# Reading the moving operand of every product in sixteens from the end, with the split weights at other addresses

## The chip, the cores and the metric

One core of a Trainium2 chip. The metric is the device time of one execution of the whole program, in microseconds; the kernel is one launch.

## The reference

Two transformer blocks for one sequence of 256 tokens and width 2048, in fp32. The first has modulation from a condition vector, a gated linear recurrence in two directions with 8 heads (after a pass over a context of 256 tokens that yields its starting states), a short gated convolution beside it, a gated merge, an output projection, and a feed-forward of width 5632 with a 3 x 3 depthwise convolution on a 64-wide grid. The second has 16 extra leading tokens (so 272), eight heads of stick-breaking attention and eight of differential attention, and an output projection. In outline:

```python
mod = silu(c) @ w_mod + b_mod
h = modulate(rms_norm(x), sh1, sc1)
z = h @ w_in                      # q, two forget gates, v, g, conv and merge gates
o = recurrence(z)                 # both directions, states from the context
merged = sigmoid(ga) * (y_a @ w_pa) + sigmoid(gb) * (y_b @ w_pb)
x = x + g1 * (merged @ w_o)
a, b = split(modulate(rms_norm(x), sh2, sc2) @ w_up)
x = x + g2 * ((silu(dwconv(a)) * b) @ w_down)
x = rms_norm(x) * final_g
proj = rms_norm(concat(meta, x)) @ w_in_2
x = x + concat(stick_breaking(proj), diff_attention(proj)) @ w_out_2
```

## The kernel before

All activations are kept with the features on the 128 partitions and the tokens along the free axis. Every large matrix is cut into units of 128 output features: one unit is 16 blocks of 128 x 128 weights (11 in the stage down), 1 MB, fetched by one DMA of the sync queue into one of four places of RAW. A unit becomes one **product**: for each of its 16 blocks three matmuls accumulate into one bank of ACC. The three are needed because an fp32 number is split in two parts of a faster type (fp32r), a high and a low one: ScalarE copies the high part of the weights from RAW to HI (line 488), VectorE writes the rest, RAW minus HI, to LO (line 1308), each in two halves and two slots that alternate from product to product. The activations were split in the same way when they were made (HX for the first block's input, YAB for the two branches, MRG for the merged one, HXU for the feed-forward's input, SH and SL for its hidden layer, U2 for the second block, MIX for its attention outputs). The three matmuls are HI with the high part, HI with the low part, LO with the high part.

The moving operand of a matmul is one block of activations: 256 columns of consecutive fp32 numbers per partition in most stages, 272 in attention's products that need the extra tokens (the others start at column 16), and two streams of 256, x and the context, in rec, 512 columns in one matmul. HX is [128, 4, 16, 256]; the streams lie two planes, 32 KB, apart.

The stages in order: mod1 (rows of the modulation, 8 x 4 units, a matmul form of its own, lines 904 to 912), with the first products of rec slipped in block by block (early_step, line 930); rec (heads 0 to 7: three products with 512 columns and one query product with 256); mix (8 heads x 4 products, and between them small matmuls of the recurrence's levels); merge (16 columns x 3 products); out (16 products, and a modulation unit on VectorE for each, lines 1314 to 1320); up (22 x 4 products; the first two interleaved by up_step, line 1135); down (8 x 8 products of 11 blocks); attn (8 heads x 8 products, of which four with 272 columns); proj (16). While the norm before up is made, spare_products (line 1121) multiplies MRG with itself.

TensorE's order is written out by hand. `prod` (line 878) waits for a free bank, for each half of LO, and for inputs where they are still being made, and issues the matmuls:

```python
o = out(k)
mm(o, HI[:, slot, k, 0:P], xh(k), start=first, stop=False)
mm(o, HI[:, slot, k, 0:P], xl(k), start=False, stop=False)
ins = mm(o, LO[:, slot, k, 0:P], xh(k), start=False, stop=last)
```

SBUF addresses are written by hand too, by `at` (line 137), in KB above a base of 8320 bytes. Taken modulo 256 bytes, the base included: HI (32 KB) and LO (49 KB) 128; HX and HXU (66.1875), YAB (100.1875), MRG (150.1875), SH (100.1875), SL (146.9375) and MIX (137.6875) 64; U2 (97.625) 0, and 64 from its column 16 on. A block of weights is 512 bytes long on each partition, a block of activations 1024 (U2: 1280).

Of the kernel before, what the change touches and what calls it, by code (L numbers as in the profile page):

```python
# [8 lines left out]
F32R = mybir.dt.float32r  # L9
# [5 lines left out]
P = 128  # L15
D = 2048
KD = D // P
T = 256
# [113 lines left out]
def build(nc, xct, metat, crow, vec, con1, con2, wts, wdown, park, outt):  # L132
    ctx = ExitStack()
    with ctx:
        base = 8320

        def at(name, kb, shape, dt=F32):
            return nc.alloc_sbuf_tensor_at(name, shape, dt, offset=base + int(kb * 1024))
# [3 lines left out]


        RAW = at("raw", 0, [P, 4, 16, P])
        HI = at("hi", 32, [P, 2, 16, P], F32R)
        LO = at("lo", 49, [P, 2, 16, P], F32R)

        HX = at("hx", 66.1875, [P, 4, KD, T], F32R)
        YAB = at("yab", 100.1875, [P, 4, HEADS, T], F32R)
# [16 lines left out]
        HXU = at("hxu", 66.1875, [P, 2, KD, T], F32R)  # L166
# [101 lines left out]
        ACC = ctx.enter_context(nc.psum_tensor("acc", [P, 4, 512], F32))  # L268
# [84 lines left out]
        def halves(ph):  # L353
            return ((0, DH), (DH, DT)) if ph == "down" else ((0, 8), (8, 16))
# [116 lines left out]
        def _(act):  # L471
# [5 lines left out]
            def hi(ph, i, p, only=(0, 1)):  # L477
# [6 lines left out]
                for h in only:  # L484
                    a, b = (halves(ph) if p < L else ((0, 8), (8, 16)))[h]
                    need = 2 if ph == "down" and p == L else h + 1
                    act.wait_ge(mm_half, 2 * (q - 2) + need)
                    A.activation(HI[:, slot, a:b, 0:P], RAW[:, p % 4, a:b, :], ACT.Copy).then_inc(hi_half, 1)  # L488

# [46 lines left out]
            for s in range(2):  # L536
                act.wait_ge(raw_early[s], 16)
                for a, b in ((0, 8), (8, 16)):
                    A.activation(HI[:, s, a:b, 0:P], RAWX[:, s, a:b, :], ACT.Copy).then_inc(hi_half, 1)
            for i in range(1, ITERS["mod1"] + 1):  # L540
# [331 lines left out]
        def _(pe):  # L872
            for one in (kd_tr, v_tr, s_mm, o_mm, ss2_mm, ss3_mm, d_sc, dv_tr, d_av, b_z, bv_tr, b_av):
                pe.sem_inc(one, 1)
            def mm(*a, **k):
                return pe.matmul(*a, **k)  # L876

            def prod(ph, i, p, xh, xl, out, groups=None, bank_wait=None, between=None,
                     lo_at=None, inputs=None, each=1, needs=None):


                q, slot = prod_index(ph, i, p), prod_index(ph, 0, p) % 2
                if bank_wait is None:
                    pe.wait_ge(bank_free, q - 3)
                elif bank_wait is not False:
                    pe.wait_ge(bank_free, bank_wait)
                n = halves(ph)[1][1]
                for h, (a, b) in enumerate(halves(ph)):
                    if h and between:
                        between()  # L890
                    pe.wait_ge(lo_half, (used(ph, i, p) if lo_at is None else lo_at) + h + 1)
                    for k in range(a, b):
                        if needs and k in needs:
                            pe.wait_ge(inputs, needs[k])
                        elif inputs and not needs and k % 4 == 0:
                            pe.wait_ge(inputs, each * (k // 4 + 1))
                        first, last = groups(k) if groups else (k == 0, k == n - 1)
                        o = out(k)
                        mm(o, HI[:, slot, k, 0:P], xh(k), start=first, stop=False)
                        mm(o, HI[:, slot, k, 0:P], xl(k), start=False, stop=False)  # L900
                        ins = mm(o, LO[:, slot, k, 0:P], xh(k), start=False, stop=last)
                    ins.then_inc(mm_half, 1)

            def rows(i, p):
# [19 lines left out]
            xch, xcl = (lambda k: HX[:, 0:3:2, k, 0:T]), (lambda k: HX[:, 1:4:2, k, 0:T])  # L924
# [5 lines left out]
            def early_step(s, k, high, low):  # L930

                if k % 8 == 0:
                    pe.wait_ge(lo_half, 2 * s + k // 8 + 1)
                o = ACC[:, s, :].rearrange("p (s t) -> p s t", s=2)
                mm(o, high, xch(k), start=k == 0, stop=False)
                mm(o, high, xcl(k), start=False, stop=False)
                ins = mm(o, low, xch(k), start=False, stop=k == KD - 1)
                if k == KD - 1:
                    ins.then_inc(mm_half, 2)

            def early(k):

                pe.wait_ge(hx_ready, k + 1)
                for s in range(2):
                    early_step(s, k, HI[:, s, k, 0:P], LO[:, s, k, 0:P])
                if k >= LAG:
# [55 lines left out]
            def rec_head(i, second=False):  # L1002

                for p in range(3):
                    prod("rec", i, 2 * p, xch, xcl, lambda k: ACC[:, p, :].rearrange("p (s t) -> p s t", s=2),
                         between=first_turns if second and p == 0 else None)
                    if second and p == 0:
                        rec_state(0)
                rec_query("rec", i, 6, lambda: rec_turns(i))
                rec_state(i)  # L1010
# [124 lines left out]
            def up_step(p, k):  # L1135

                slot = prod_index("up", 0, p) % 2
                if k % 8 == 0:
                    pe.wait_ge(lo_half, used("up", 0, p) + k // 8 + 1)
                o = ACC[:, p, 0:T]  # L1140
                mm(o, HI[:, slot, k, 0:P], HXU[:, 0, k, 0:T], start=k == 0, stop=False)
                mm(o, HI[:, slot, k, 0:P], HXU[:, 1, k, 0:T], start=False, stop=False)
                return mm(o, LO[:, slot, k, 0:P], HXU[:, 0, k, 0:T], start=False, stop=k == KD - 1)

            pe.wait_ge(bank_free, prod_index("up", 0, 1) - 3)
            for n in range(KD + BEHIND):
                if n < KD:
# [4 lines left out]
                    ins = up_step(0, n)  # L1152
                    if n % 8 == 7:
                        ins.then_inc(mm_half, 1)
                if n >= BEHIND:
                    ins = up_step(1, n - BEHIND)
# [11 lines left out]
            with pe.Fori(0, ITERS["down"]) as i:  # L1168
                for jj in range(2):
                    for q in range(4):  # L1170
                        p = 4 * jj + q
                        u = prod_index("down", i, p)
                        if jj == 0:
# [3 lines left out]
                             bank_wait=u - 4 if q == 0 else False)  # L1177
# [13 lines left out]
            def attn_head(i, peeled):  # L1191

                def proj(p, meta, between=None, inputs=None, needs=None, bank_wait=None):

                    a = 0 if meta else NMETA
                    prod("attn", i, p, lambda k: U2[:, 0, k, a:TA], lambda k: U2[:, 1, k, a:TA],
                         lambda k: ACC[:, p % 4, 0:TA - a], between=between, inputs=inputs, needs=needs,
                         bank_wait=bank_wait)

                def tokens_major(src, bank):  # L1200

# [4 lines left out]
                if peeled:  # L1206
                    proj(0, False, between=last_squares, inputs=u2_ready, needs={k: k + 1 for k in range(KD)},
                         bank_wait=PROD0["attn"] - 4)
# [22 lines left out]
                for c in range(2):  # L1231
                    r = slice(64 * c, 64 * c + 64)
                    mm(AUX[:, c, 0:P + NMETA], DQK[r, 0, NMETA:NMETA + P], DQK[r, 1, 0:P + NMETA], start=True, stop=True)
                    ins = mm(AUX[:, c, P + NMETA:P + NMETA + TA], DQK[r, 0, NMETA + P:TA], DQK[r, 1, :], start=True, stop=True)
# [4 lines left out]
                for key, (a, q, w) in enumerate(SBQ):  # L1239
                    ins = mm(AUX[:, 1, a:a + w], SKF[:, key * P:(key + 1) * P], SQF[:, q:q + w], start=True, stop=True)  # L1240
# [44 lines left out]
            with pe.Fori(0, ITERS["proj"]) as i:  # L1285
                for p in range(4):
                    prod("proj", i, p, lambda k: MIX[:, 0, k, 0:T], lambda k: MIX[:, 1, k, 0:T], lambda k: ACC[:, p, 0:T],
                         inputs=mix_ready, needs=head_order if p == 0 else {KD: 0})
# [3 lines left out]
        def _(dve):  # L1292
# [6 lines left out]
            def lo(ph, i, p, only=(0, 1)):  # L1299
# [5 lines left out]
                for h in only:  # L1305
                    a, b = (halves(ph) if p < L else ((0, 8), (8, 16)))[h]
                    dve.wait_ge(hi_half, 2 * s + h + 1)
                    V.tensor_tensor(LO[:, slot, a:b, 0:P], RAW[:, p % 4, a:b, :], HI[:, slot, a:b, 0:P].bitcast(F32),  # L1308
                                    ALU.subtract).then_inc(lo_half, 1)
# [74 lines left out]
            for s in range(2):  # L1384
                for h, (a, b) in enumerate(((0, 8), (8, 16))):
                    dve.wait_ge(hi_half, 2 * s + h + 1)
                    if s or h:
                        dve.wait_ge(lo_half, 2 * s + h)
                    V.tensor_tensor(LO[:, s, a:b, 0:P], RAWX[:, s, a:b, :], HI[:, s, a:b, 0:P].bitcast(F32),
                                    ALU.subtract).then_inc(lo_half, 1)  # L1390
# [687 lines left out]
```

## Time and profile before

| | us |
|---|---|
| three runs | 2258.78, 2259.56, 2261.01 |
| median | 2259.56 |
| profiled execution, from first to last instruction | 2259.2 |
| TensorE busy | 2223.9 (98%), 18451 matmuls |
| weight loads busy | 2143.9 (95%) |
| VectorE busy | 1633.3 (72%) |
| ScalarE busy | 995.8 (44%) |
| mean granted clock of TensorE | 0.996 |

The profile's page gives one execution. Its span differs from the runs' times only by what lies around the first and last instruction, here less than the spread of the runs. A matmul's recorded duration runs until its last result is out, so consecutive ones overlap: the rate is to be read from their starts, or from a long stretch divided by the number of matmuls in it. Weight loads (PEld) run beside matmuls.

### The profile page before, as it was taken

Reading aid. Unit: us, or ns where it says so; the run is one execution under the profiler, and the core shown is the slowest. Engines: PE = TensorE matmul, PEld = TensorE weight load, DVE = VectorE, ACT = ScalarE, POOL = GpSimd, SP = SyncE. Lnnn points to the kernel's source line nnn. Section 1 sums busy time; section 2 is a strip of 40 time slices with the busy share of each in tenths; the row PEclk is TensorE's granted clock in tenths of the full one; section 3 lists DMA queues with packets and bytes.
Section 4 is the critical chain, followed back from the end, with each engine's and each line's share of the span. In section 5 each row is a group of like instructions: output and inputs, shape, how many; then the busy total and the mean of one; then the engine's idle time right before and its main releaser. Section 6 shows DMA issues by size and latency. Waiting matters only on the chain.

```text
span 2259.2 us, 48355 instructions
## 1 busy us (share of the span) xinstructions
PE 2223.9 (98%) x18451; PEld 2143.9 (95%) x18451; DVE 1633.3 (72%) x2523; ACT 995.8 (44%) x1402; POOL 8.4 (0%) x18
## 2 busy tenths in 40 slices
PE   5999999999999999999999999999999999999999
PEld 4788888999999999999999999999999999999999
DVE  4465565899987666998888888875656766767764
ACT  4332222565543333454444444444445444444453
POOL 0000000000000000000000000000000000000000
PEclk8999999999999999999999999999999999999999
DMA  9955565444468766894555555556556444444443
GB/s 404 401 228 206 197 233 191 168 149 149 149 225 312 284 257 239 339 354 169 200 192 199 188 186 198 194 211 202 189 185 233 150 152 165 149 154 162 149 177 139
DMA packets 69519, 475.73 MB, mean 211 GB/s; under 512 B 7728, under 2 KB 9776, under 8 KB 18384
## 3 DMA queue, kind: packets, MB, share of 16 engines
q1 hardware_dynamic: 68688, 467.59, 56.1%
q0 software_dynamic: 768, 7.26, 0.9%
q8 instruction: 44, 0.72, 0.1%
q14 instruction: 19, 0.16, 0.0%
HBM read 469.58 MB, written 5.24 MB: 210 GB/s over the span
## 4 chain that ended last, share of the span: by engine, by line
PE 93%; DMA 4%; DVE 2%; ACT 1%; issue 0%; SPq 0%; DVEq 0%; ACTq 0%
PE acc L876 87%; PE aux L876 5%; DMA raw<-wts 4%; DVE lo L1308 1%; PE aux L1203 0%; DVE cv L1744 0%; DVE n L1688 0%; ACT hi L488 0%; PE aux L979 0%; PE aux L973 0%; DVE raw L1318 0%; DVE u L1772 0%; PE aux L1250 0%; DVE hxu L1325 0%; PE aux L1252 0%
## 5 line engine op out<-in xcount | busy, mean ns | idle before, releaser
L1308 DVE TENSOR_TENSOR lo<-raw,hi 128x1024 fp32r<-128x1024 f32 (+1 forms) x714 | 810.0, 1168 | 185.0 <-ACT hi L488 180.3
L488 ACT ACTIVATE hi<-raw 128x1024 fp32r<-128x1024 f32 (+1 forms) x714 | 693.8, 1012 | 299.9 <-PE acc L876 235.2
L876 PE MATMUL acc<-hx,hi 128*128 128x256 f32 (+1 forms) x3040 | 648.4, 311 | 1.3 <-DVE hx L1371 1.3
L876 PEld LDWEIGHTS acc<-hx,hi 128*128 128x128 f32 x3040 | 488.8, 189 | 37.1 <-issue 2.4
L876 PE MATMUL acc<-hxu,hi 128*128 128x256 f32 x2816 | 479.8, 276 | 0.5 <-DVE lo L1308 0.3
L876 PE MATMUL acc<-hx,lo 128*128 128x256 f32 (+1 forms) x1520 | 468.1, 308 | 0.0
L876 PEld LDWEIGHTS acc<-hxu,hi 128*128 128x128 f32 x2816 | 424.1, 188 | 1.6 <-DVE hxu L1325 1.1
L876 PE MATMUL acc<-hxu,lo 128*128 128x256 f32 x1408 | 388.7, 276 | 0.0
L876 PE MATMUL acc<-u,hi 128*128 128x272 f32 (+1 forms) x2048 | 381.6, 288 | 0.0
L876 PEld LDWEIGHTS acc<-u,hi 128*128 128x128 f32 x2048 | 318.1, 189 | 4.3 <-issue 2.5
L876 PEld LDWEIGHTS acc<-hx,lo 128*128 128x128 f32 x1520 | 287.9, 189 | 16.7
L876 PE MATMUL acc<-u,lo 128*128 128x256 f32 (+1 forms) x1024 | 291.1, 284 | 0.0
L876 PEld LDWEIGHTS acc<-hxu,lo 128*128 128x128 f32 x1408 | 264.3, 188 | 0.0
L876 PE MATMUL acc<-sh,hi 128*128 128x256 f32 x704 | 194.3, 276 | 0.0
L876 PE MATMUL acc<-sl,hi 128*128 128x256 f32 x704 | 194.3, 276 | 0.0
L876 PE MATMUL acc<-sh,lo 128*128 128x256 f32 x704 | 194.3, 276 | 0.0
L876 PEld LDWEIGHTS acc<-u,lo 128*128 128x128 f32 x1024 | 192.7, 188 | 0.0
L876 PEld LDWEIGHTS acc<-sh,hi 128*128 128x128 f32 x704 | 132.2, 188 | 0.0
L876 PEld LDWEIGHTS acc<-sl,hi 128*128 128x128 f32 x704 | 132.2, 188 | 0.0
L876 PEld LDWEIGHTS acc<-sh,lo 128*128 128x128 f32 x704 | 132.2, 188 | 0.0
L1744 DVE SCALAR_TENSOR_TENSOR cv<-at,vec,cv 128x256 f32<-128x256 f32 x308 | 129.5, 480 | 0.0
L876 PE MATMUL acc<-yab,hi 128*128 128x256 f32 x512 | 91.2, 281 | 0.3 <-DVE lo L1308 0.3
(301 smaller groups left out, 2327.0 us busy)
## 6 DMA issues: line engine op xcount, KB each, us to landing
raw<-wts SPq DMA_DIRECT2D x389, 1024.0 KB, 4.8
raw<-wdown SPq DMA_DIRECT2D x64, 704.0 KB, 4.1
xc<-xct SPq DMA_DIRECT2D x1, 4096.0 KB, 12.6
rawx<-wts SPq DMA_DIRECT2D x2, 1024.0 KB, 24.3
x<-xct SPq DMA_DIRECT2D x1, 2048.0 KB, 11.1
park<-x POOLq DMA_DIRECT2D x1, 2048.0 KB, 9.6
xf<-park POOLq DMA_DIRECT2D x1, 2048.0 KB, 9.0
outt<-outs SPq DMA_DIRECT2D x16, 128.0 KB, 3.4
```

Of the source, the lines that this page charges most:

```text
L488: A.activation(HI[:, slot, a:b, 0:P], RAW[:, p % 4, a:b, :], ACT.Copy).then_inc(hi_half, 1)
L876: return pe.matmul(*a, **k)
L1308: V.tensor_tensor(LO[:, slot, a:b, 0:P], RAW[:, p % 4, a:b, :], HI[:, slot, a:b, 0:P].bitcast(F32), ALU.subtract).then_inc(lo_half, 1)
L1744: mark(V.scalar_tensor_tensor(acc4[n % 2], a, w, acc4[n % 2], ALU.mult, ALU.add))
```

## The change

The moving operand and the output of a product's matmul are read and written in another order of columns. `paired`, for one block of 256 columns, cuts it into its two halves and each half into eight runs of sixteen; it goes through the runs from the last to the first and takes from each step the run of the first half, then that of the second. `streams`, for 512 columns, cuts each stream into sixteen runs, goes from the last to the first and takes at each step the run of the first stream, then that of the second. Since the moving operand and the output are reordered alike, every result lands where it was. Attention's 272-column products keep their order, as do the spare products, the rows of mod1 and all small matmuls. HI lies 64 bytes higher and LO 192 bytes lower.

```diff
-        HI = at("hi", 32, [P, 2, 16, P], F32R)
-        LO = at("lo", 49, [P, 2, 16, P], F32R)
+        HI = at("hi", 32.0625, [P, 2, 16, P], F32R)
+        LO = at("lo", 48.8125, [P, 2, 16, P], F32R)
...
+            def paired(x):
+
+                return x.rearrange("p (b a c) -> p a b c", b=2, c=16)[:, ::-1]
+
+            def streams(x):
+
+                return x.rearrange("p s (a c) -> p a s c", c=16)[:, ::-1]
+
             def prod(ph, i, p, xh, xl, out, groups=None, bank_wait=None, between=None,
-                     lo_at=None, inputs=None, each=1, needs=None):
+                     lo_at=None, inputs=None, each=1, needs=None, order=paired):
...
-                        o = out(k)
-                        mm(o, HI[:, slot, k, 0:P], xh(k), start=first, stop=False)
-                        mm(o, HI[:, slot, k, 0:P], xl(k), start=False, stop=False)
-                        ins = mm(o, LO[:, slot, k, 0:P], xh(k), start=False, stop=last)
+                        o, high, low = order(out(k)), order(xh(k)), order(xl(k))
+                        mm(o, HI[:, slot, k, 0:P], high, start=first, stop=False)
+                        mm(o, HI[:, slot, k, 0:P], low, start=False, stop=False)
+                        ins = mm(o, LO[:, slot, k, 0:P], high, start=False, stop=last)
...
```

`early_step` and the three 512-column products of `rec_head` use `streams`, `up_step` uses `paired`, in the same manner, and attention's `proj` passes `order=(lambda x: x) if meta else paired`.

## Rows read from the trace of the kernel before

**Rows 1.** The page: busy times, the chain by engine and line, LO's group.

```profile
PE 2223.9 (98%) x18451; PEld 2143.9 (95%) x18451; DVE 1633.3 (72%) x2523; ACT 995.8 (44%) x1402; POOL 8.4 (0%) x18
...
PE 93%; DMA 4%; DVE 2%; ACT 1%; issue 0%; SPq 0%; DVEq 0%; ACTq 0%
PE acc L876 87%; PE aux L876 5%; DMA raw<-wts 4%; DVE lo L1308 1%; PE aux L1203 0%; DVE cv L1744 0%; DVE n L1688 0%; ACT hi L488 0%; PE aux L979 0%; PE aux L973 0%; DVE raw L1318 0%; DVE u L1772 0%; PE aux L1250 0%; DVE hxu L1325 0%; PE aux L1252 0%
...
L1308 DVE TENSOR_TENSOR lo<-raw,hi 128x1024 fp32r<-128x1024 f32 (+1 forms) x714 | 810.0, 1168 | 185.0 <-ACT hi L488 180.3
```

**Rows 2.** Chain in order of time: start, length, what, matmuls (rec, mix, merge, out, up/down, proj).

```profile
166.56 36.42 PE acc L876 x168
...
533.10 2.74 PE acc L876 x24
536.28 2.83 PE acc L876 x24
...
652.21 260.31 PE acc L876 x2208
...
935.36 68.60 PE acc L876 x580
...
1042.37 690.70 PE acc L876 x6092
...
2169.48 87.16 PE acc L876 x768
```

**Rows 3.** Busy time by window: mod1, mix, merge, out, up.

```profile
core 0: us, PE busy (x) PEld busy (x) DVE busy (x) ACT busy (x) POOL busy (x), PEclk, DMA share, GB/s
0.00:106.00 106.00, 77.03 (x1185) 59.01 (x1186) 46.33 (x98) 38.59 (x57) 0.20 (x4) 0.92 0.97 402
500.00:700.00 200.00, 199.74 (x1718) 199.11 (x1718) 181.59 (x293) 110.22 (x187) 2.64 (x5) 1.00 0.51 188
660.00:900.00 240.00, 240.00 (x2040) 240.00 (x2040) 168.13 (x198) 93.69 (x112) 0.00 (x0) 1.00 0.74 280
937.00:1003.00 66.00, 66.00 (x563) 66.00 (x562) 63.10 (x72) 29.79 (x37) 0.00 (x0) 1.00 0.98 379
1100.00:1300.00 200.00, 200.00 (x1768) 200.00 (x1767) 169.59 (x296) 93.31 (x128) 0.00 (x0) 1.00 0.53 191
```

**Rows 4.** Timeline of TensorE in merge: start us, length us, instruction, how many.

```profile
799.62 0.40 PE L876 MATMUL acc<-hx,hi 128*128 128x256 f32 x2
799.86 0.28 PE L876 MATMUL acc<-hx,lo 128*128 128x256 f32 x1
799.98 0.40 PE L876 MATMUL acc<-hx,hi 128*128 128x256 f32 x2
```

**Rows 5.** Timeline of TensorE in up.

```profile
1399.84 0.39 PE L876 MATMUL acc<-hxu,hi 128*128 128x256 f32 x2
1400.07 0.28 PE L876 MATMUL acc<-hxu,lo 128*128 128x256 f32 x1
1400.18 0.39 PE L876 MATMUL acc<-hxu,hi 128*128 128x256 f32 x2
```

**Rows 6.** Timeline of TensorE at the spare products.

```profile
1006.82 2.20 PE L876 MATMUL acc<-mrg 128*128 128x256 f32 x17
1008.86 0.40 PE L876 MATMUL acc<-hxu,hi 128*128 128x256 f32 x2
```

**Rows 7.** Timeline of TensorE at a head's transposes in rec.

```profile
129.29 0.60 PE L973 MATMUL aux<-con,exc 128*128 128x128 f32 x4
129.72 0.60 PE L979 MATMUL aux<-con,vs 128*128 128x128 f32 x4
```

**Rows 8.** Timeline of the weight loads in mod1; a load's mean duration (page).

```profile
66.37 0.97 PEld L876 LDWEIGHTS aux<-vec,row 128*128 128x128 f32 x8 [0.20 <-issue]
...
L876 PEld LDWEIGHTS acc<-hx,hi 128*128 128x128 f32 x3040 | 488.8, 189 | 37.1 <-issue 2.4
```

**Rows 9.** Groups of TensorE by shape: busy us, mean ns of one.

```profile
L876 PE MATMUL acc<-hxu,lo 128*128 128x256 f32 x1408 | 388.7, 276 | 0.0
L876 PE MATMUL acc<-u,hi 128*128 128x256 f32 x1024 | 185.1, 284 | 0.0
L876 PE MATMUL acc<-u,lo 128*128 128x256 f32 x512 | 142.8, 279 | 0.0
```

**Rows 10.** Timeline of TensorE at attention's 272-column products.

```profile
1743.88 0.42 PE L876 MATMUL acc<-u,hi 128*128 128x272 f32 x2
1744.14 0.29 PE L876 MATMUL acc<-u,lo 128*128 128x272 f32 x1
1744.26 0.42 PE L876 MATMUL acc<-u,hi 128*128 128x272 f32 x2
```

More of the change, by code:

```diff
@@ L933, in early_step @@
                     pe.wait_ge(lo_half, 2 * s + k // 8 + 1)
[L934 to L937, printed above, removed]
+                o = streams(ACC[:, s, :].rearrange("p (s t) -> p s t", s=2))
+                mm(o, high, streams(xch(k)), start=k == 0, stop=False)
+                mm(o, high, streams(xcl(k)), start=False, stop=False)
+                ins = mm(o, low, streams(xch(k)), start=False, stop=k == KD - 1)
                 if k == KD - 1:
@@ L1005, in rec_head @@
                     prod("rec", i, 2 * p, xch, xcl, lambda k: ACC[:, p, :].rearrange("p (s t) -> p s t", s=2),
-                         between=first_turns if second and p == 0 else None)
+                         between=first_turns if second and p == 0 else None, order=streams)
                     if second and p == 0:
@@ L1139, in up_step @@
                     pe.wait_ge(lo_half, used("up", 0, p) + k // 8 + 1)
[L1140 to L1143, printed above, removed]
+                o, high, low = (paired(x) for x in (ACC[:, p, 0:T], HXU[:, 0, k, 0:T], HXU[:, 1, k, 0:T]))
+                mm(o, HI[:, slot, k, 0:P], high, start=k == 0, stop=False)
+                mm(o, HI[:, slot, k, 0:P], low, start=False, stop=False)
+                return mm(o, LO[:, slot, k, 0:P], high, start=False, stop=k == KD - 1)
             pe.wait_ge(bank_free, prod_index("up", 0, 1) - 3)
@@ L1197, in proj @@
                          lambda k: ACC[:, p % 4, 0:TA - a], between=between, inputs=inputs, needs=needs,
-                         bank_wait=bank_wait)
+                         bank_wait=bank_wait, order=(lambda x: x) if meta else paired)
                 def tokens_major(src, bank):
```

## The prediction, made before the changed kernel had run

> **What bounds the kernel now.** I read the page first. TensorE is busy in 98% of the span, and the chain that ended last is 93% TensorE, 87% of it the line of the product matmuls [rows 1]. So the question isn't which engine waits but at what rate the products follow each other. The busy time and the mean duration don't answer this, since one matmul lasts longer than the distance to the next. I took the distance from the chain in order of time, where long stretches hold products alone [rows 2]: up and down give 690.70 / 6092 = 113.4 ns a matmul, the last projection 87.16 / 768 = 113.5, merge 260.31 / 2208 = 117.9, out 68.60 / 580 = 118.3. In mix both rates occur: half a product (24 matmuls) takes 2.74 or 2.83 us, 114 or 118 ns, 116 in the mean. In rec a piece holds 144 matmuls of 512 columns and 24 of 256; with 117.9 for the latter, (36.42 - 2.83) / 144 = 233.3 ns.
>
> 256 columns at the full clock of 2.4 GHz, which is granted in every window from 500 us on [rows 3], are 106.7 ns. The timelines show steady trains: hx three from 799.62 to 799.98 us (0.36, so by the chain 117.9 each), hxu three from 1399.84 to 1400.18 (0.34, 113.3 each) [rows 4, 5]. Both have one shape, one pair of HI and LO slots and one address of the moving operand (HX and HXU both start at 66.1875 KB). So 6.7 or 11.1 ns a matmul are neither columns nor the clock. VectorE isn't the cause either: its busy share is 70% at the slow rate and 85% at the fast [rows 3]. A third rate comes from the spare products at line 1124, whose weights and moving operand lie in MRG 1024 bytes apart: 17 in 2.04 us, 120.0 ns [rows 6]. My reading is that the moving read and the read of the next weights, which runs beside it for nearly the whole matmul (in merge the loads are busy in 240 of 240 us [rows 3]), get in each other's way, and how often depends on addresses and on the phase in which the trains have locked.
>
> **How low a matmul can go.** Four transposes of 128 columns take 0.43 us, 108 ns each [rows 7]. Eight weight loads with only two moving columns behind each span 0.97 us; less the last one's 0.19 (a load lasts 189 ns), seven distances are 0.78, or 111 ns [rows 8]. The weight load alone sets about this. I take 110 ns as the floor for 256 columns. For 512 I add the same 3.3 ns to 213.3: 216.7.
>
> **What the change does, in addresses.** HI moves by +64 bytes, LO by -192. Modulo 256 bytes both are +64, and 256 bytes are four runs of sixteen fp32 numbers. All moving operands that are reordered (HX, YAB, MRG, HXU, SH, SL, MIX, and U2 from column 16) start at the same place modulo 256: 64, against 128 for the weights before and 192 after. Half of a 256-column operand is 512 bytes, so with the new order both reads of a pair have the same place modulo 256, and the stream steps down by 64 bytes in every 32 columns. The weight load takes 128 columns in the time of 256 moving ones, thus also 64 bytes in 32 columns. If the weights are read from their end, the two reads then keep a constant distance. If they are read from their start, they meet more often than now. No row tells the direction.
>
> **Part by part.**
> 1. Reordered 256-column products, by stage (a product is 16 blocks of three, 48 matmuls; projection and the rest from the loops). Up and down: 4224 + 2112 = 6336 x (113.4 - 110) = 21.5 us. Last projection: 768 x 3.5 = 2.7. Merge and out: 2304 + 768 = 3072 x 7.9 = 24.3. Mix: 1536 x 6 = 9.2. Query products of rec: 384 x 7.7 = 3.0. Attention's 256-column ones: the durations say 279 for LO where hxu has 276 [rows 9]; duration less distance is 276 - 113.3 = 163, so 116, and hi is higher through first matmuls; 1536 x 6 = 9.2. Sum 69.9.
> 2. Streams of 512 columns in rec, seven heads of three products: 1008 x (233.3 - 216.7) = 16.7. The 144 early ones in mod1 lie in the first 106 us for the most part, where the DMA is 97% busy and moves 402 GB/s [rows 3]: nothing. Together 86.6.
> 3. The 1536 matmuls of 272 columns keep their order but get the new weight address. Now three take 0.38 us, 126.7 [rows 10], which is 119.2 for 256 columns. Bounds: 272 / 2.4 + 3.3 = 116.7 (15 us less) and the spare products' 120.0 scaled to 127.5 (1 us more). I take zero, as the row lies at the top end and nothing in their order changes.
> 4. The switches between runs of sixteen, in the moving read and in PSUM. A 256-column matmul gets 15 of them, a 512-column one 31. Before, the only such switch is the one between the two streams, and its price can't be told from the rest of the 19.9 ns over 213.3. Lower bound zero; upper bound a cycle each, 6.3 ns, since that is as large as the whole loss of a 113.3 ns matmul. I take zero, because the 512-column train with its one switch loses 0.039 ns a column, between the fast trains without one (0.026) and the slow (0.043), and so gives no sign of a price; the upper end stays for the range.
> 5. ScalarE's and VectorE's instructions on HI and LO are the same in number and shape; only the address differs. Zero, covered by the matmuls. Where the cover is thinnest, in out, a product has two LO instructions of 1168 ns [rows 1]; were the new address to make them a tenth longer, that would be 0.23 us x 16 = 3.7 us there and nothing elsewhere.
> 6. What becomes late next. Out: VectorE is busy in 63.10 of 66 us and DMA 98% [rows 3]. A product there takes 48 x 0.1183 = 5.68 us, of which VectorE needs 5.43; TensorE at 110 would want 5.28. So 16 x 0.15 = 2.4 us come back as waits for LO. Mix: VectorE is busy in 181.59 of 200 us, so a 5% shorter head leaves it at 95%; I put 3 us for the level tiles that arrive late. Rests: 1 us. Together 6.4.
>
> Sum: 86.6 - 6.4 = 80 us off the profiled execution, whose span is 2259.2 and so 0.4 below the median of the runs, 2259.56. That makes 2179.5; I say 2180.
>
> **The skill against the rows.** The Trainium skill, TensorE: Matmul & The Clock Gate, section "Step-by-step: what each phase is for", says that TensorE has two independent read ports and that loading the next weights takes no bandwidth from the running matmul. By that rule no order of reading gains anything, and the sum would be zero, the third rival below. The rows speak against it, as one shape at one clock runs at 113.3, 117.9 and 120.0 ns.
>
> **Rivals.**
> - *The 113.3 is a floor.* The fast rate is the same in up, down and projection to 0.1 ns over thousands of matmuls, which looks more like a fixed hand-over than like clashes. Then only the slow trains come down to it: merge and out 3072 x 4.6 = 14.1, mix 1536 x 2.7 = 4.1, rec queries 384 x 4.6 = 1.8, attention 1536 x 2.7 = 4.1, streams at twice 113.3: 1008 x 6.7 = 6.7. Sum 31, time 2229. Against it: weight loads at 111 and transposes at 108. Chance 0.21.
> - *Each switch costs.* Place: every reordered matmul. At one cycle (0.42 ns) a switch and with the clashes left as they are, 13632 x 6.25 = 85 and 1008 x 12.9 = 13: 98 us more, 2357. It decides from about 0.4 ns a switch on, where it eats the gain of part 1 (69.9 us / 13632 = 5.1 ns, 15 switches). For it: no row shows such short runs. The same end is reached if the weights are read from their start and the reads meet oftener: the spare products' 120.0 on all of them would add 7104 x 6.6 = 47 in up, down and projection, 3456 x 2.1 = 7 in merge, out and rec, and 3072 x 4 = 12 in mix and attention, 66 in all, 2326. Together 0.23. Beside it, in the skill: Advanced Engine Details and Errata, section "PSUM Cachelines", says that any non-contiguous pattern slows matmuls markedly but also that two consecutive elements suffice for the best rate; by the first half it comes out slower, by the second runs of sixteen are free. No row here decides.
> - *It does nothing.* The lock is elsewhere (in the hand-over between instructions) and order and address don't touch it: 2259. The mixed rates in mix at equal addresses speak for some such thing. Chance 0.07.
>
> **Numbers.** Forecast as summed 0.49, its own range 2158 to 2205 (floor of 108, with the 272-column gain in part, to a floor of 111.4 and more waits). With the second case at 2229 and no change at 2259 this is 0.77; the range runs to 2290 to take the mild part of the slower case. This kernel's measurement can tell about 0.2%, 4.5 us, from no change. Faster: 0.49 + 0.21, less a little where a small switch price eats it, 0.69. Same 0.07. Slower 0.24.
>
> **What would show it.** Right: the merge stretch of 2208 products takes near 243 us instead of 260.31, up and down near 670 instead of 690.70, both at one rate; mean durations fall from 276 and 281 to about 273; the spare products stay at 120.0; VectorE waits for TensorE less, TensorE for LO in out a little more. Wrong: hxu still at 113.3 with hx come down to it (the floor), or hxu at 118 or more (the switches). If 272-column trains move, the address alone has an effect.

## The result, and the profile after

The changed kernel takes 2275.11 us (median of four runs, 2274.72 to 2276.2) against 2259.17 for the kernel before (four runs, 2249.98 to 2261.01). The ratio is 1.0081, interval 1.0058 to 1.0105: slower by 0.8%, where 2180 had been forecast. One remark for reading the numbers: the 51 runs of the kernel before, the later ones included, fall into groups near 2250 (23 runs), 2260 (17), 2276 (5) and 2286 us (6), so the changed kernel's 2275 lies above the two groups that hold 40 of them, at the third and below the fourth.

The profiled execution has a span of 2274.4 us, 15.2 more than before. Its page, in the lines that answer to [rows 1] (busy times, VectorE's LO group):

```profile
PE 2235.2 (98%) x18451; PEld 2160.4 (95%) x18451; DVE 1632.2 (72%) x2523; ACT 995.0 (44%) x1402; POOL 8.4 (0%) x18
...
L1316 DVE TENSOR_TENSOR lo<-raw,hi 128x1024 fp32r<-128x1024 f32 (+1 forms) x714 | 809.6, 1167 | 189.4 <-ACT hi L488 184.5
```

TensorE has work in 98% of the span as before, LO's duration is unchanged, and the numbers of instructions are the same. So the 15 us lie in the rate of the products, and the chain in order of time tells in which stage (start, length, what, matmuls; answers to [rows 2]):

```profile
168.28 35.69 PE acc L876 x168
...
649.93 39.45 PE acc L876 x336
695.92 8.36 DMA raw<-wts
706.67 201.88 PE acc L876 x1728
...
931.39 66.03 PE acc L876 x580
...
1008.98 737.62 PE acc L876 x6318
...
2182.10 89.71 PE acc L876 x768
```

Length by number gives the distance from one matmul to the next. Merge: 201.88 / 1728 = 116.8 ns, where it was 117.9. Out: 66.03 / 580 = 113.8 (118.3). Up and down: 737.62 / 6318 = 116.7 (113.4). Projection: 116.8 (113.5). In rec 24 of the 168 have 256 columns: (35.69 - 2.80) / 144 = 228.4 (233.3). The windows show the same by their counts (stretches of merge, out and up; answers to [rows 3]):

```profile
core 0: us, PE busy (x) PEld busy (x) DVE busy (x) ACT busy (x) POOL busy (x), PEclk, DMA share, GB/s
710.00:900.00 190.00, 190.00 (x1631) 190.00 (x1630) 125.95 (x147) 75.78 (x91) 0.00 (x0) 1.00 0.71 264
937.00:995.00 58.00, 58.00 (x514) 58.00 (x514) 56.78 (x66) 26.68 (x33) 0.00 (x0) 1.00 0.99 390
1100.00:1300.00 200.00, 200.00 (x1717) 200.00 (x1716) 164.01 (x286) 90.34 (x125) 0.00 (x0) 1.00 0.53 189
```

In up 1717 matmuls fit into 200 us, where 1768 did. TensorE is busy in 100% of the window both times, at the full granted clock: neither number tells that the engine got slower. A stage that had run at the best rate lost it. Single starts in up (timeline of TensorE: start, length, instruction, how many), to compare with [rows 5]:

```profile
1199.85 0.39 PE L876 MATMUL acc<-hxu,hi 128*128 128x256 f32 x2
1200.08 0.28 PE L876 MATMUL acc<-hxu,lo 128*128 128x256 f32 x1
1200.19 0.39 PE L876 MATMUL acc<-hxu,hi 128*128 128x256 f32 x2
```

The groups by shape (busy us, mean ns of one; answers to [rows 9]) say it too. The lo matmuls of hxu went from 276 to 279 ns, those of 272 columns stand at 289 (290 before):

```profile
L876 PE MATMUL acc<-hxu,lo 128*128 128x256 f32 x1408 | 392.2, 279 | 0.0
...
L876 PE MATMUL acc<-u,lo 128*128 128x272 f32 x512 | 147.9, 289 | 0.0
```

**The balance**, from the times at which the same piece begins or ends in both chains: rec's first long piece begins 1.7 us later than before (168.28 for 166.56). The last of rec's pieces ends 2.35 us earlier (405.27 for 407.62), so rec gained 4.1. Mix lost 0.1. Merge ends 3.97 earlier (908.55 for 912.52), a gain of 1.7: 2304 x 1.1 = 2.5, less a short wait for weights, which shows as the DMA piece at 695.92. Out ends 6.54 earlier (997.42 for 1003.96), a gain of 2.6. The projection begins 12.62 later (2182.10 for 2169.48): up, attention and down lost 19.2. Of this, up and down lost 20.1 (down ends at 1746.60 for 1733.07), which 6336 x 3.33 = 21.1 explains but for a microsecond, and attention gained 0.9. The projection loses 2.55. The sum is 1.7 - 4.1 + 0.1 - 1.7 - 2.6 + 19.2 + 2.6, or 15.2.

### The profile page after: what moved, and what is told of

The parts are those of the page before. It is cut to its first block, busy times and chain, and to the rows that moved or that the text cites. A ratio compares the mean times of both kernels' runs of the same rounds, so it can differ in the third digit from the quotient of the medians.

```text
span 2274.4 us, 48355 instructions
## 1 busy us (share of the span) xinstructions
PE 2235.2 (98%) x18451; PEld 2160.4 (95%) x18451; DVE 1632.2 (72%) x2523; ACT 995.0 (44%) x1402; POOL 8.4 (0%) x18
## 4 chain that ended last, share of the span: by engine, by line
PE 92%; DMA 4%; DVE 2%; ACT 0%; issue 0%; SPq 0%; DVEq 0%; ACTq 0%
PE acc L876 87%; PE aux L876 5%; DMA raw<-wts 4%; DVE lo L1316 1%; PE aux L1211 0%; DVE raw L1326 0%; ACT hi L488 0%; DVE n L1696 0%; PE aux L981 0%; PE aux L987 0%; DVE u L1780 0%; PE aux L1258 0%; DVE hxu L1333 0%; PE aux L1067 0%; PE aux L1260 0%
## 5 line engine op out<-in xcount | busy, mean ns | idle before, releaser
L1316 DVE TENSOR_TENSOR lo<-raw,hi 128x1024 fp32r<-128x1024 f32 (+1 forms) x714 | 809.6, 1167 | 189.4 <-ACT hi L488 184.5
L876 PE MATMUL acc<-hxu,hi 128*128 128x256 f32 x2816 | 493.6, 279 | 0.3 <-DVE hxu L1333 0.2
L876 PEld LDWEIGHTS acc<-hxu,hi 128*128 128x128 f32 x2816 | 429.5, 188 | 1.1 <-DVE hxu L1333 0.9
```

## Experiments

All distances below are length by number from the chain in order of time, or differences of starts in a timeline. A train is an unbroken row of products. The *upper* rate of a train is the slower one, with the larger distance.

**e1, e2: the two halves of the change, each alone.** e1 moves only the weights' halves:

```
-        HI = at("hi", 32, ...)    LO = at("lo", 49, ...)
+        HI = at("hi", 32.0625, ...)    LO = at("lo", 48.8125, ...)
```

> Columns in the old order, HI and LO at the new addresses. Clash theory (how often the moving read and the weight read meet depends on order and distance together): the trains of hxu leave 113.3 ns, most likely upwards towards 117.8, the 272-column ones leave 126.7; time between 2240 and 2300. Switch theory (runs of sixteen cost by themselves): all as before, hxu at 113.3, hx at 117.8, 2259. Lock theory (the rate is one of a few that a train falls into when it starts): rates out of the set 113.3, 117.8, 120 and mixed from stage to stage.

e2 is the changed kernel with HI and LO back at 32 and 49, so only the order is new.

> Columns in the new order, HI and LO at the old addresses. Switch theory: same rates as in the changed kernel, 116.7 ns in merge, up, down and projection, 228.8 for 512 columns, 2275. Clash theory: another distance gives another rate, 117 to 124 ns, time 2280 to 2370. Lock theory: 116.7 or 113.3 by stage, but not in the same stages as in the changed kernel.

Measured: e1 2307.13 us (two runs), ratio 1.0139, 1.0016 to 1.0263. e2 2286.96 us (eight runs, five near 2286 and three near 2303), ratio 1.014, 1.0086 to 1.0194. Chain of e1 (rec, merge, up and down):

```profile
167.00 36.44 PE acc L876 x168
...
655.76 262.27 PE acc L876 x2208
...
1021.56 749.87 PE acc L876 x6316
```

and of e2 (rec, merge, up and down):

```profile
166.06 35.48 PE acc L876 x168
...
704.27 203.04 PE acc L876 x1728
...
1010.37 741.66 PE acc L876 x6317
```

The addresses alone put every 256-column train at 118.7 to 118.8 ns and leave the streams at 233.3. The order alone puts them at 117.3 to 117.5 and the streams at 226.8. The spans are 46.6 and 24.6 us over that of before, while both edits together cost 15.2: they don't add. So both the address and the order enter the rate, but with either alone no long train came down to the 113.3 that the kernel before had in up, down and projection.

**e3, e4: is it the step down, or the pairing?** e3 walks the sixteens upward, e4 takes them downward without alternating between the halves:

```
-                return x.rearrange("p (b a c) -> p a b c", b=2, c=16)[:, ::-1]
+                return x.rearrange("p (b a c) -> p a b c", b=2, c=16)      # e3
+                return x.rearrange("p (a c) -> p a c", c=16)[:, ::-1]      # e4
```

and likewise in the order of the streams.

> The changed kernel with the runs taken from the first to the last, still alternating between halves or streams. Clash theory with weights read from their end: the two reads now run against each other and meet often, over 120 ns a matmul, 2320 or more; with weights read from their start: fewer meetings, under 113.3 ns, 2230 or less. Switch theory: the direction is nothing to it, 116.7 ns and 2275.

> The changed kernel with the runs from the end but one half (or stream) after the other, so the moving read steps down twice as fast as the weights' 64 bytes in 32 columns. Clash theory: the distance is no longer constant, 117.8 to 120 ns for 256 columns and over 233 for 512, 2285 to 2310. Switch theory: as many switches as in the changed kernel, 116.7 ns and 2275.

Measured: e3 2332.63 us, ratio 1.0251 (1.0127 to 1.0376); e4 2327.7, ratio 1.023 (1.0105 to 1.0355); two runs each. Chain of e3 in rec, and in merge and out in one piece:

```profile
168.31 37.45 PE acc L876 x168
...
665.77 357.90 PE acc L876 x2980
```

357.90 / 2980 = 120.1 ns, and e4 has the same there (357.88 for 2980). The streams are at (37.45 - 2.88) / 144 = 240.1 ns in e3 and, from e4's 36.96 for 168, at 236.7. Both the descent and the pairing are needed to get from 120.0 to 116.7. So the order of the reads matters, and not the number of switches alone: e3 and e4 have the changed kernel's fifteen in each matmul and are 3.3 ns slower than it.

**e5: is 113.3 a stable property of the kernel before?** The kernel before again, with no edit.

> The kernel before, unchanged, profiled again. Its runs so far lie between 2249 and 2287. Lock theory (a train of equal matmuls falls at its start into one of two rates, 113.3 or 117.8 ns, and keeps it): runs differ by sums of whole stages, up and down together 6336 x 4.4 = 28 us, merge 10, out and projection 3 each; the profile shows a stage at another rate than in the first profile, with nothing between 113.3 and 117.8 in a long train. Rival (the spread comes from something else, such as the DMA or the start): every stage at the rate of the first profile, 113.3 in up and down and 117.8 in merge, and the difference in waits.

Ten runs, 2248.56 to 2286.26, median 2251.67; ratio 0.999 (0.9958 to 1.0022). The profile has the stages of the first: merge 260.31 us for 2208, up and down 690.69 for 6092. The second profile agrees with the first, but both are of executions in the group near 2260, and the ten spread by 1.7%; e12 takes this up.

**e6, e7: another address.** HI at 32.125 and LO at 48.875 (64 bytes beyond the change), in the old order (e6) and in the new (e7).

> The kernel before with HI 128 bytes higher and LO 128 lower, so both +128 modulo 256; columns in the old order. Clash theory: the rate follows from the distance between the two reads, so a third value beside 113.3 or 117.8 at +0 and 118.7 at +64: 117 to 120 ns, 2290 to 2330. If the distance is nothing to it: 113.3 or 117.8 and 2249 to 2287.

> The changed kernel with HI 128 bytes above its old place and LO 128 below, columns in the new order. Clash theory with weights read from their end: at a constant distance some distances meet all the time and some never; +0 gave 117.3 and +64 gave 116.7 ns, so +128 is either clear, 110 to 113.3, 2230 or less, or a collision course, over 120, 2330 or more. Switch theory: 116.7 as in the changed kernel, 2275.

e6: 2253.45 and 2290.27 us in two runs. e7: 2274.01 (eight runs, 2273.03 to 2274.6), ratio 1.0067 (1.0027 to 1.0106). Chain of e6 (merge, projection):

```profile
649.04 250.50 PE acc L876 x2208
...
2158.54 90.56 PE acc L876 x768
```

Here the old order has merge at 250.50 / 2208 = 113.5 and the projection at 117.9: the reverse of before. Up begins at 117.8 and goes on at 113.3. e7 has 116.7 in merge, up, down and projection. The pieces of rec of e6, where no order was edited:

```profile
206.30 35.69 PE acc L876 x168
```

That is the length of the changed kernel's. By the starts, the streams have 228.9 ns here in the old order, 228.4 in e7 and 228.4 in the changed kernel: at this address the old order of streams is within 0.5 ns of the new. One order, one address and one shape thus show two rates in one execution, as [rows 4, 5] did for different operands. Old order: 113.3 or 117.8. New order: 116.7 in these stages, neither clear nor a collision course; the switch theory has the number, but e3 and e4 with as many switches had 120.0.

**e8: the streams alone.** The changed kernel with `paired` returning its argument and HI, LO at 32, 49: only the 512-column order is new.

> The kernel before with the new order in the 512-column products alone, HI and LO at their old places. With the new order at these addresses 512 columns took 226.7 ns in place of 233.3, so 1008 x 6.6 = 6.7 us less in rec whatever the theory. Lock theory: the rest falls into its two rates by run, 2243 to 2280, so the gain is hard to see in the runs and plain in rec's rate. Switch theory: 31 switches a matmul make rec slower, more than 233.3 ns.

Measured: 2244.65 us (ten runs, 2242.57 to 2253.92), ratio 0.9953 (0.9916 to 0.999) against 25 runs of before, whose median is 2258.94. This is faster than both kernels. Chain (rec, merge, up and down, projection):

```profile
165.60 35.40 PE acc L876 x168
...
645.24 250.50 PE acc L876 x2208
...
1023.95 690.69 PE acc L876 x6092
...
2151.06 87.16 PE acc L876 x768
```

Up, down and projection are back at 113.4 to the hundredth of a microsecond ([rows 2] have 690.70 and 87.16). The streams gain: (35.40 - 2.72) / 144 = 226.9. Merge came out at 113.5 for 117.9, though nothing in it was edited. So of the 18.4 us between the spans 9.8 are merge's, whose lower rate also occurs with no order edited (e6), and some 1.7 out's; the streams give 1008 x 6.5 = 6.6 us. The lowest run, 2242.57, is 5.4 under the lowest of before.

**e9: both reads held in place.** In merge, up, down and projection the moving operand is sixteen columns read sixteen times, or the weights one column read 128 times:

```
+ moving:  x[:, 16*place : 16*place+16].unsqueeze(1).broadcast_to([P, 16, 16])
+ weights: w[:, 0:1].broadcast_to([P, P])
```

Merge: both held at the same place modulo 256. Up: both held, 128 bytes apart. Down: only the moving one. Projection: only the weights, with the columns read upward as in the kernel before.

> The changed kernel, with the addresses of the reads pinned in four stages (their results are not the reference's; the number of matmuls, their shape and all waits stay). Merge: moving operand always columns 32 to 47 of its block, weights always column 0, the same place modulo 256 bytes. Up: moving operand always columns 0 to 15, weights always column 0, 128 bytes apart modulo 256. Down: moving pinned, weights swept as before. Projection: weights pinned, moving swept upwards. Clash theory: up runs free at its floor, near 110 ns as the prediction had it; merge, where the two always meet, far above 120; down and projection between. Floor theory (113.3 is 17/16 of 106.7, a loss that belongs to the matmul itself and not to a meeting): up, down and projection at 113.3 and merge no different. Switch theory: the pinned streams have 15 jumps back a matmul, so 116.7 or more in up, down and merge, and 113.3 or 117.8 in the projection.

2315.27 us, one run. Windows in merge, up, down and projection:

```profile
700.00:900.00 200.00, 200.00 (x1653) 200.00 (x1653) 129.06 (x155) 77.95 (x93) 0.00 (x0) 1.00 0.70 262
1100.00:1300.00 200.00, 200.00 (x1639) 200.00 (x1638) 156.67 (x274) 87.41 (x120) 0.00 (x0) 1.00 0.51 178
1550.00:1750.00 200.00, 200.00 (x1646) 200.00 (x1645) 109.56 (x138) 84.42 (x114) 0.00 (x0) 1.00 0.55 179
2240.00:2300.00 60.00, 60.00 (x532) 60.00 (x531) 29.80 (x33) 23.33 (x22) 0.00 (x0) 1.00 0.52 182
```

121.1, 122.2, 121.7 and 113.3 ns (from the starts). If the reads clashed when their places modulo 256 met, one of the first two should have been much worse than the other; they are 1.1 ns apart, and both are slower than every order tried up to here. That speaks against my picture of places modulo 256. The floor theory's 113.3 holds in the projection and fails in up and down.

**e10: the length of the runs.** The same paired descent in runs of 32 (merge), 8 (up), 4 (down), and plainly backward (projection).

> The changed kernel with another length of run in four stages: 32 columns in merge, 8 in up, 4 in down, and in the projection no halves and every column from the last to the first. Results are the reference's. Switch theory at 16 columns costs 116.7 - 113.3 = 3.3 ns for 15 switches, so 0.22 ns a switch: merge 115, up 120, down 127, projection 113.3 or far above 150. Clash theory: the mean speed of the stream through the addresses is the same for 32, 8 and 4, so up and down stay at 116 to 118 and merge too; the projection steps down twice as fast as the weights, 117 to 120.

2344.31 us, one run. Windows in merge, up, down and projection:

```profile
700.00:900.00 200.00, 200.00 (x1683) 200.00 (x1683) 130.68 (x155) 78.58 (x94) 0.00 (x0) 1.00 0.70 261
1100.00:1300.00 200.00, 200.00 (x1581) 200.00 (x1581) 149.87 (x262) 84.43 (x116) 0.00 (x0) 1.00 0.49 176
1550.00:1750.00 200.00, 200.00 (x1581) 200.00 (x1580) 103.86 (x132) 80.21 (x108) 0.00 (x0) 1.00 0.55 185
2260.00:2330.00 70.00, 70.00 (x586) 70.00 (x585) 33.51 (x38) 25.94 (x25) 0.00 (x0) 1.00 0.47 165
```

119.0 for 32, 126.7 for 8 and the same 126.7 for 4, 120.0 for backward. A price per switch would double from 8 to 4 and be halved at 32; neither happened. Each length was run in one stage only, from one start. Sixteen is the best of these lengths, with 116.7 in these stages.

**e11, e12: is the rate fixed by order and address, or by how a train starts?** Ahead of each product in up stand one to four small matmuls (16 columns, into a bank not in use; the profile records each as two), in the changed kernel (e11) and in the kernel before (e12):

```
-                up_units(i, range(4))
+                for p in range(4):
+                    for _ in range(p + 1):
+                        mm(AUX[:, 3, 0:16], ONESR[:], ONESR[:, 0:16], start=True, stop=True)
+                    up_units(i, (p,))
```

> The changed kernel with one, two, three and four small fp32 matmuls (16 columns, into an unused bank) ahead of the four products of every turn of up's loop, so that each product's train starts anew, 84 starts in all. Lock theory: within up the new order runs at 116.7 in some products and at 113.3 in others, the same order at the same addresses, and down keeps one of the two for its whole length. Rival (the rate follows from order and addresses alone, 116.7 in this stage): 116.7 after every start. The knocks themselves cost some 84 x 2.5 x 0.2 = 42 us.

> The same small matmuls in the kernel before. Lock theory: within up the old order runs at 117.8 in some products and at 113.3 in others. Rival: 113.3 after every start, as in all profiles of the old order so far. With this and the run of the changed kernel with knocks: if the share of fast starts is far larger in the old order, the loss of the change in up and down is one of where the trains fall, not of what the order costs.

2321.75 and 2323.2 us, one run each. What counts is inside. Timeline of TensorE in e12 (the small matmuls are the `aux` lines; a product of 48 begins at the `hxu,hi` line):

```profile
1083.19 0.48 PE L876 MATMUL acc<-hxu,hi 128*128 128x256 f32 x2
...
1088.93 0.52 PE L876 MATMUL aux<-onesr 128*128 128x16 f32 x4
1089.29 0.48 PE L876 MATMUL acc<-hxu,hi 128*128 128x256 f32 x2
...
1094.82 0.74 PE L876 MATMUL aux<-onesr 128*128 128x16 f32 x6
1095.40 0.48 PE L876 MATMUL acc<-hxu,hi 128*128 128x256 f32 x2
...
1100.93 0.96 PE L876 MATMUL aux<-onesr 128*128 128x16 f32 x8
1101.74 0.48 PE L876 MATMUL acc<-hxu,hi 128*128 128x256 f32 x2
...
1107.48 0.29 PE L876 MATMUL aux<-onesr 128*128 128x16 f32 x2
```

The four products last 5.74, 5.53, 5.53 and 5.74 us. The difference, 0.21 / 48 = 4.4 ns a matmul, is that of 117.8 and 113.3. It goes with the number of small matmuls ahead (one and four: slow; two and three: fast), in 83 of the 84 products by the starts inside them. Down, with no edit, ran at 117.8 in this execution, and not at 113.3:

```profile
1541.69 253.59 PE acc L876 x2153
```

This fits the groups in which the runs of before fall. Merge at the one rate or the other is 2208 x 4.44 = 9.8 us, up and down 6092 x 4.44 = 27.1: from 2250 that gives 2260, 2277 and 2287. It is an estimate, as both profiles of that kernel are of the group near 2260. The same in e11:

```profile
1084.19 0.48 PE L876 MATMUL acc<-hxu,hi 128*128 128x256 f32 x2
...
1089.89 0.74 PE L876 MATMUL aux<-onesr 128*128 128x16 f32 x6
1090.47 0.48 PE L876 MATMUL acc<-hxu,hi 128*128 128x256 f32 x2
...
1096.16 0.96 PE L876 MATMUL aux<-onesr 128*128 128x16 f32 x8
```

5.70 and 5.69 us, and so on: by the starts inside them all 84 products run at 116.7 ns. The old order falls to its fast or its slow rate by how the train starts; with the new order these starts all gave one rate, nearer to the slow one.

**e13, e14: the reading side or the writing side?** e13: up reads in the new order and writes in the old, down the reverse; in merge and projection the weights are held on one column. e14: e11 with all writes in the old order.

```
+            def in_place(x):
+                return x.rearrange("p (a b c) -> p a b c", b=2, c=16)
```

> The changed kernel with the two halves of the change of order taken apart (results are not the reference's). Up: moving operand read in the new order, output written in the old. Down: read in the old order, written in the new. Merge and projection: new order on both sides, weights pinned to one column. If the read side counts: up at 116.7, down at 118.7 as with the new addresses alone. If the write side counts: up at 118.7, down at 116.7. If the weights' sweep is what holds the new order at 116.7: merge and projection at 113.3 with pinned weights; if it is the order alone: 116.7 there too.

> The changed kernel with the small matmuls of the earlier knock run in up, and every 256-column product read in the new order but written in the old (results are not the reference's). With both sides new, all starts in up fell to 116.7; with the read side alone new, up was at 113.3 after its first 200 matmuls. Written side costs: 113.3 after most or all starts, and merge, down and projection at 113.3 too. Chance of the start alone: 116.7 after most starts here as well, and the 113.3 of the run before was luck.

e13: 2265.9 us. Merge and projection are at 116.7 with the weights held (257.85 us for 2208; 89.70 for 768), so their sweep isn't what sets that rate. Down, new order only in the writes, 118.7. Up ran at 116.7 for its first 200 matmuls or so and at 113.3 after a start at 1034.9 us. Window in up:

```profile
1100.00:1300.00 200.00, 200.00 (x1767) 200.00 (x1767) 168.22 (x294) 94.57 (x130) 0.00 (x0) 1.00 0.54 195
```

1767 in 200 us: the new order can run at 113.3 too, as it does in out of the changed kernel (113.8; in e7, e9, e10, e11, e13 and e14 the same stage has 117.1 to 117.2). e14: 2321.84 us, span 2320.1 against 2320.0 in e11, with up, merge, down and projection at 116.7 as there. The order of the writes alone thus makes no difference here. What e13 shares with e14 in up is the edit, and what it doesn't share is the start, so the 113.3 goes with the start.

**e15: old order, weights held, with the small matmuls.** e12 with each block's weights in merge and up read from one column.

> The kernel before with the same small matmuls in up, and the weights of merge and up pinned to one column (results are not the reference's). With swept weights half of the starts in up fell to 117.8 and half to 113.3. If the two rates come from the moving read meeting the weights' sweep: 113.3 after every start and in merge. If they come from the hand-over of instructions, whatever is read: 117.8 after half of the starts again.

2319.03 us. Timeline of TensorE in up:

```profile
1083.77 0.48 PE L876 MATMUL acc<-hxu,hi 128*128 128x256 f32 x2
...
1089.31 0.51 PE L876 MATMUL aux<-onesr 128*128 128x16 f32 x4
1089.67 0.48 PE L876 MATMUL acc<-hxu,hi 128*128 128x256 f32 x2
...
1095.51 0.74 PE L876 MATMUL aux<-onesr 128*128 128x16 f32 x6
```

5.54 and 5.84 us, 113.3 and 120.0 ns: fast after an odd number of small matmuls, slow after an even one, in 83 of 84 products. Merge, held too, has a third rate, 257.86 / 2208 = 116.8:

```profile
652.37 257.86 PE acc L876 x2208
```

More than one rate remains when the weights are read from one place; the upper one in up moved from 117.8 to 120.0. So what makes the rates isn't a meeting of two sweeps, while how the weights are read shifts the upper one.

## Why the prediction was wrong

**The step that failed: the floor of 110 ns.** It rested on transposes of 128 columns at 108 ns [rows 7] and weight loads with two moving columns at 111 [rows 8], other kinds of work than the products, of which I took one property, the distance. In the 17 profiles no train of 256-column products ran under 113.3 ns, at three pairs of addresses and in eight orders of reading, and no stream of 512 under 226.7, which is twice that. (113.3 is 106.7 x 17/16; why is not shown.) So part 1 gave 24.2 us to up, down and projection, which had nothing to gain. The rival "113.3 is a floor" said this, on a row that I had: one rate, to 0.1 ns, over thousands of matmuls. I gave more weight to two rows of other operations.

**The second: that a rate belongs to an order and an address.** The rival too let every slow train come down to 113.3. e12 shows that one stage, one order and one address run at 113.3 or 117.8 by how the train starts, and e13 shows the same for the new order with 113.3 and 116.7. The change pulled the upper rate down from 117.8 to 116.7, and it pulled up, down and projection, 7104 matmuls that before mostly ran on the lower rate, to the upper. 7104 x 3.33 = 23.7 us, against some 9 us that rec, merge, out and attention gained: that is the sign of the result. The rest of part 1 was over-sized by the same two errors: merge gained 1.7 us of 18, out 2.6 of 6, mix nothing of 9 (its products went from 115.9 to 116.6 ns in the mean), attention 0.9 of 9. "The phase in which the trains have locked" stood in the prediction's reading, but no term of the sum and no rival let a fast train be moved to a slow phase.

**Part 2**, the streams: right in direction, 4.9 ns a matmul where 16.7 us meant 16.6 ns; floor again (226.7 is the lowest seen). The new order of streams is the one part that pays (e8), and at the weights' old addresses: e6 has most of the gain, 228.9, with no order changed.

**Parts 3 and 5** held: 272 columns at 126.6 both times (by the starts; at the third pair of addresses 125.9 in e6 and 125.3 in e7); LO 1167 ns after 1168. **Part 6**, waits for LO in out, was just not reached: out ran at 113.8, or 5.46 us a product where VectorE needs 5.43, and VectorE was busy in 56.78 of 58 us.

**Part 4**, switches at zero: not contradicted as a price per switch. With e3, e4 and e10 the distance follows no count of switches. The rival "each switch costs" had the sign of the result right and its mark (hxu at 118 or more) not: e2 117.3 and the changed kernel 116.7. The floor's mark (hxu still at 113.3) failed too. The rest of this rival, reads that meet oftener, isn't shown either (e9, e13, e15).

**My reading of the cause**, two reads that get in each other's way by their place modulo 256, is half right. Order and address of the reads matter: 113.3 to 126.7 ns for one shape at one clock. By the rule of the Trainium skill that I had set against it (TensorE: Matmul & The Clock Gate, "Step-by-step: what each phase is for": loading the next weights takes nothing from the running matmul) the weights' address should have been nothing to the rate. It wasn't: with the address alone new, up went to 118.7, which is neither of the old order's two rates (e1). But in e13 and e15 there are slow trains still where the weights' sweep is taken away, so no run shows that the weight load is what takes the time, and the rule itself isn't refuted. The other rule, Advanced Engine Details and Errata, "PSUM Cachelines": its first half (any non-contiguous pattern slows matmuls) doesn't hold for writes in runs of 16, e14 with contiguous writes having the span of e11 to 0.1 us.

Against a meeting of places also speaks that the distances within a slow train repeat in a period of their own. In up and merge of the changed kernel they go about 115, 120, 117, 115 ns, again every four matmuls, in e1 and e2 every five, while the addresses modulo 256 are the same for every matmul and the three operands of a block come round every three.

**Open.** What the rates are, what in a start chooses one, and why the new order nearly always chooses the upper one. The number of small matmuls steers it (e12, e15), but no rule here says which number gives which rate, and no run measured the queue between load and matmul by itself.

## What to carry to other kernels

Measure a matmul train by the distance between starts (length by number in the chain, or the count in a window), since the busy share hides the 4% between 113.3 and 117.8 ns and the mean duration shows only 3 to 5 ns of 280. A back-to-back train of products with a weight load each can have several stable rates for the same code: before trading on one, look which trains already have the best, and take it that an edit can lose it there; look at several profiles and every stage. Change the order where it showed a gain (two streams of 512 columns, e8), not wherever it can be applied, try a plain move of an address first (e6), and take a floor only from rows of the same kind of matmul.

## What the runs showed of the hardware that was not expected

- Rates are few and sharp: 113.3, 116.7, 117.3, 117.8, 118.7, 119.0, 120.0, 126.7 ns for 256 columns at the full granted clock; a train keeps its rate for up to thousands of matmuls (6092 at 113.4).
- Each of them fits a whole number of steps of 6.67 ns (106.7 / 16 ns, an estimate worked out from these rates) over a few matmuls: 113.3 is 17 steps, 120.0 is 18, 116.7 is 70 over four, 117.8 is 53 over three, 117.3 and 118.7 are 88 and 89 over five, 126.7 is 38 over two, and 119.0 in e10 is 232 over thirteen. What beats at that step isn't shown.
- One to four matmuls of 16 columns ahead of a product change the following 48 by 4.4 ns each (e12), and by 6.7 with the weights read from one column (113.3 and 120.0; e15).
- Reading the same sixteen columns over and over with held weights is slower (121.1, 122.2) than reading 256 different ones upward with held weights (113.3, e9).
- Trains with runs of 8 and of 4 columns have the same distance, 126.7; with runs of 16 it was 116.7 and, from some starts, 113.3.
- The Trainium skill, TensorE: Matmul & The Clock Gate, section "Wait — 56ns, not 53.3ns?", gives columns by 2.4 GHz plus 2.5 ns for back-to-back matmuls. For 256 columns that is, as an estimate from it, 109.2 ns. No product train here came nearer than 113.3.
